# A two-block transformer step on one core: matmul operand tiles and split-weight slots get strides of 2096 and 4112 bytes

## What is computed

```python
h_l = modulate(rms_norm(x, g_mix_norm[l]), sh_a, sc_a)
qa_l, kva_l, kr_l, cb_l, cc_l, ch_l = split_projection(h_l @ w_in[l])
...
x = x + gt_a * merge_heads(att_l, conv_l, g_mix_out[l], w_out[l])
hf_l = modulate(rms_norm(x, g_ffn_norm[l]), sh_f, sc_f)
x = x + gt_f * conv_ffn(hf_l, w_up[l], ffn_conv_w[l], ffn_conv_b[l], w_down[l])
...
z = hn @ w_in
...
x = x + merged @ w_out
hm = rms_norm_2(x, norm_mlp_g)
x = x + jnp.square(jax.nn.relu(hm @ w_up)) @ w_down
```

## Time and profile before

| | |
|---|---|
| median of 2 runs | 2871.82 us (2871.63 to 2872.02) |
| the profiled execution's own time | 2872.42 us |
| its span in the trace | 2870.6 us |
| TensorE, matmuls (PE) | busy 2684.6 us, 94%, 21408 entries |
| TensorE, weight loads (PEld) | busy 2571.9 us, 90% |
| VectorE (DVE) | busy 1794.6 us, 63% |
| ScalarE (ACT) | busy 1224.7 us, 43% |
| DMA | 552.93 MB, mean 193 GB/s |
| mean granted TensorE clock | 0.959 of full speed |

### The profile page before, as it was taken

The page is one execution under the profiler, slowest core; times in us unless marked ns, Lnnn a source line. Parts: engine busy times, 40 slices in busy tenths (PEclk is TensorE's granted clock), DMA queues, the critical chain, the costliest instruction groups (busy, mean ns, idle before and its releaser), DMA issues.

```text
span 2870.6 us, 52211 instructions
## 1 busy us (share of the span) xinstructions
PE 2684.6 (94%) x21408; PEld 2571.9 (90%) x21408; DVE 1794.6 (63%) x2056; ACT 1224.7 (43%) x1407; POOL 20.8 (1%) x24
## 2 busy tenths in 40 slices
PE   4959977768899999999999999999999999999998
PEld 3659975348899999999999999999999999999998
DVE  3988965678766776576556455555555555555554
ACT  2733331223455554354454344444444443434433
POOL 0000000000000000000000000000000000000000
PEclk9989987769999999999999899999999999999999
DMA  4958953427566656656556455566556666666562
GB/s 156 384 195 315 331 171 120 147 88 282 188 191 201 195 182 204 192 163 220 183 171 186 130 173 166 161 188 199 196 178 184 191 197 192 190 196 193 196 206 103
DMA packets 288834, 552.93 MB, mean 193 GB/s; under 512 B 19434, under 2 KB 28632, under 8 KB 288024
## 3 DMA queue, kind: packets, MB, share of 16 engines
q1 hardware_dynamic: 287416, 548.10, 59.2%
q10 hardware_dynamic: 1248, 2.42, 0.3%
HBM read 548.35 MB, written 2.10 MB: 192 GB/s over the span
## 4 chain that ended last, share of the span: by engine, by line
PE 86%; DVE 9%; issue 2%; ACT 2%; DMA 1%; ACTq 1%; DVEq 0%; SPq 0%
PE half L1627 25%; PE half L1629 25%; PE half L1628 25%; DVE wlo L909 2%; PE half L1683 1%; DVE acc L931 1%; PE half L1661 1%; PE half L1663 1%; DVE acc L928 1%; PE half L1662 1%; DVE tmp L1233 1%; DMA raw<-in_w_ada 1%; PE half L1832 1%; PE half L1821 1%; PE half L1822 1%
## 5 line engine op out<-in xcount | busy, mean ns | idle before, releaser
L909 DVE TENSOR_TENSOR wlo<-raw,whi 128x1024 fp32r<-128x1024 f32 (+2 forms) x917 | 1096.7, 1209 | 815.8 <-ACT whi L511 813.6
L511 ACT ACTIVATE whi<-raw 128x1024 fp32r<-128x1024 f32 (+2 forms) x917 | 952.5, 1048 | 1195.0 <-PE half L1629 1033.6
L1627 PE MATMUL half<-hf,whi 128*128 128x256 f32 x2400 | 663.9, 277 | 6.2 <-DVE hf L986 5.1
L1628 PE MATMUL half<-hf,whi 128*128 128x256 f32 x2400 | 663.4, 276 | 0.0
L1629 PE MATMUL half<-hf,wlo 128*128 128x256 f32 x2400 | 663.4, 276 | 0.0
L1627 PE MATMUL half<-hid,whi 128*128 128x256 f32 x1712 | 474.0, 277 | 0.0
L1628 PE MATMUL half<-hid,whi 128*128 128x256 f32 x1712 | 473.4, 276 | 0.0
L1629 PE MATMUL half<-hid,wlo 128*128 128x256 f32 x1712 | 473.4, 276 | 0.0
L1627 PEld LDWEIGHTS half<-hf,whi 128*128 128x128 f32 x2400 | 451.4, 188 | 7.0 <-issue 5.5
L1629 PEld LDWEIGHTS half<-hf,wlo 128*128 128x128 f32 x2400 | 451.3, 188 | 0.0
L1628 PEld LDWEIGHTS half<-hf,whi 128*128 128x128 f32 x2400 | 451.2, 188 | 0.0
(11 more groups left out here) (253 smaller groups left out, 3092.0 us busy)
## 6 DMA issues: line engine op xcount, KB each, us to landing
raw<-in_w_up SPq DMA_DIRECT2D x288, 512.0 KB, 4.4
raw<-in_w_in SPq DMA_DIRECT2D x216, 512.0 KB, 4.1
raw<-in_w_down SPq DMA_DIRECT2D x212, 512.0 KB, 4.1
raw<-in_w_ada SPq DMA_DIRECT2D x192, 512.0 KB, 5.7
raw<-in_w_out SPq DMA_DIRECT2D x64, 512.0 KB, 4.7
raw<-in_w_proj_a SPq DMA_DIRECT2D x16, 512.0 KB, 3.7
raw<-in_w_proj_b SPq DMA_DIRECT2D x16, 512.0 KB, 4.2
raw<-in_w_up SPq DMA_DIRECT2D x16, 384.0 KB, 3.5
```

The lines of the kernel that those rows point to most:

```text
L511: A(whi[:, s, 0:elems], raw[:, c, 0:elems], ACT.Copy).then_inc(s_hi_ready, 1)
L909: V.tensor_tensor(wlo[:, s, 0:elems], raw[:, c, 0:elems], whi[:, s, 0:elems].bitcast(F32), ALU.subtract).then_inc(s_drained, 1)
L1627: mm(o, hi, x[:, 0:T], start=(k == 0 and b % 2 == 0), stop=False, skip_group_check=True)
L1628: mm(o, hi, x[:, T:2 * T], start=False, stop=False, skip_group_check=True)
```

## The change

`SKEW` (12 elements, 48 bytes) is added to the row of each block k of the ten moving-operand tiles, and `SLOT_SKEW` (4 elements, 16 bytes) to each slot of `whi` and `wlo`. The added elements are never written or read. The stride from k to k + 1 becomes 2096 bytes and the one from slot to slot 4112 bytes. Since `whi` and `wlo` grow by 64 bytes each, `wlo` starts 64 bytes later (82112) and all behind it 128 bytes later; tiles that lie behind a skewed one move further (`hf` and `h2` at 124864, `hid0` at 158400, `hid1` and `merged` at 191936). The instructions of every engine, their order, counts, shapes and waits are the same ones; only addresses differ. `raw`, into which the DMAs write, keeps its place and stride, and `qn` and `kvn` keep their strides.

```diff
+SKEW = 12
+SLOT_SKEW = 4
...
-        whi = sb("whi", [P, NSPLIT, CW], F32R)
-        wlo = sb("wlo", [P, NSPLIT, CW], F32R)
+        whi = sb("whi", [P, NSPLIT, CW + SLOT_SKEW], F32R)
+        wlo = sb("wlo", [P, NSPLIT, CW + SLOT_SKEW], F32R)
...
-        h1 = sb("h1", [P, KT, 2 * T], F32R, scope=sc)
+        h1 = sb("h1", [P, KT, 2 * T + SKEW], F32R, scope=sc)
...
-        hctx = sb("hctx", [P, KT, 2 * T], F32R, scope=sc2)
+        hctx = sb("hctx", [P, KT, 2 * T + SKEW], F32R, scope=sc2)
...
-        mix = sb("mix", [P, KT, 2 * T], F32R, scope=sc)
+        mix = sb("mix", [P, KT, 2 * T + SKEW], F32R, scope=sc)
...
-        hf = sb("hf", [P, KT, 2 * T], F32R, scope=sc)
-        hid = [sb(f"hid{i}", [P, HT, 2 * T], F32R, scope=sc) for i in range(2)]
+        hf = sb("hf", [P, KT, 2 * T + SKEW], F32R, scope=sc)
+        hid = [sb(f"hid{i}", [P, HT, 2 * T + SKEW], F32R, scope=sc) for i in range(2)]
...
-        h2 = sb("h2", [P, KT, 2 * T], F32R, scope=sc)
-        heads2 = [sb(f"heads2_{i}", [P, HEADS, 2 * T], F32R, scope=sc) for i in range(2)]
+        h2 = sb("h2", [P, KT, 2 * T + SKEW], F32R, scope=sc)
+        heads2 = [sb(f"heads2_{i}", [P, HEADS, 2 * T + SKEW], F32R, scope=sc) for i in range(2)]
...
-        merged = sb("merged", [P, KT, 2 * T], F32R, scope=sc2)
+        merged = sb("merged", [P, KT, 2 * T + SKEW], F32R, scope=sc2)
```

## The result

The changed kernel takes 2949.35 us (2948.81 to 2949.88) against 2871.82 us: a ratio of 1.027, with a 95% interval of 1.0226 to 1.0314. The forecast was 2835 us, and the range ended at 2910.

A forecast was written before the change was run, and what follows sets the result against it. Behind 758 us the matmul count times their distance was taken as the bound. Fast matmuls gaining 25 us and slow ones 12, with all else zero, gave 2872.4 less 37, 2835 us; range 2786 to 2910.

The forecast's parts named there:

- What bounds the kernel: Behind 758 us, time is the number of matmuls times the distance between two starts; ahead of it TensorE shares the bound.
- The costs put at zero: DMA writes to raw, and ScalarE and VectorE writing and reading skewed slots: zero cost.
- the pair from which the prediction took its -7 to +7 ns: VectorE instructions of one size: 1218 ns on sq, 32 bytes off a multiple of 64, 1225 ns on xt.
- the term of the distances: Products behind 758 us: skewed addresses hinder load and stream less, all go at 111.7 ns, gaining 37 us.
- The two ends of the term: Products behind 758 us: 109.0 ns everywhere gains 82 us; the slow distance everywhere costs 67 us.
- 111.7 ns of the 8-column matmuls: Distance of full-clock matmuls with almost no stream beside the load, taken as the forecast for all products.
- The rival "no change": Loads set the pace and the rest is a handshake that knows no address: 2872 us, chance 0.30.
- The rival "slower": Operands fetched in 64-byte lines, skewed stretches touch one more: 85 us, 2957 us; chance 0.16 for 2939 to 2957.
- the seventeenth line: 1024 bytes starting inside a 64-byte line touch 17 lines instead of 16; the extra one costs 6.7 ns.
- the case beside it: The skew knocks every product into the slow distance: 2939 us, within the 0.16 for 2939 to 2957.
- The floor: Skill's N/2.4 + 2.5 ns, 109.2 ns for 256 columns; trace said to disagree at 113.3; best end 79 us by it.
- The range: From 2786 us, just under the full gain, to 2910, half way to the slow distance everywhere plus a little.

The follow-up runs named there:

- the whole-line skew: Both skews set to 64 bytes, where the changed kernel has 48 and 16; 2946.66 us, ratio 1.0234 to the kernel before.

## Why the prediction was wrong, point by point

**What bounds the kernel** was right. Behind 758 us the time is the number of matmuls times their distance, and 4.4 ns on each is the whole 75 us. The early stages moved by 1.7 us.

**The costs put at zero** were right. The splits on VectorE and ScalarE with skewed slots take 1223 and 1059 ns as before. It is these rows that show it; the pair from which the prediction took its -7 to +7 ns is weaker than it says, since `xt<-tmp,xt` reads `tmp`, which also lies 32 bytes off a multiple of 64.

```profile
L911 DVE TENSOR_TENSOR wlo<-raw,whi 128x1024 fp32r<-128x1024 f32 x880 | 1067.2, 1223 | 874.8 <-ACT whi L513 872.7 <-issue 0.4
...
L513 ACT ACTIVATE whi<-raw 128x1024 fp32r<-128x1024 f32 x880 | 925.5, 1059 | 1230.9 <-PE half L1631 1072.8 <-PE half L1665 55.7 <-DMA raw<-in_w_in 34.4
```

**The step that failed** is the term of the distances: "If loads and streams hinder each other when they are in the same part of a 64-byte line, then they do it now at each matmul and will do it afterwards at some of them." That took the present standing of the operands for the worst one, and from it came the gain of 37 us, where the runs show a loss of 75. They do hinder each other by address, but the kernel before has its moving tiles 64 bytes (modulo 128) from the weights, and none of the eight standings that were tried was better; its opposite, 0, costs 120.0 ns. All skews by 16 to 64 bytes lost. The two ends of the term, -82 us and +67 us, were read from rows rightly, and the 67 us (everything at the slow distance) came close to the loss. The choice between them was the error: 111.7 ns of the 8-column matmuls is what a load costs with hardly a stream beside it, and says nothing of what a stream adds elsewhere. The 8-column matmuls still follow at 111.7 ns in the timeline of the changed kernel, twelve steps in 1.34 us:

```profile
1650.58 0.25 PE L1973 MATMUL half<-whi,h 128*128 128x8 f32 x1
...
1651.92 0.25 PE L1973 MATMUL half<-whi,h 128*128 128x8 f32 x1
```

There were hints. The fast pace held for thousands of matmuls in a row, and 88% of all products had it, so there was much to lose and little to win: 1.7 ns down to the load alone, 4.5 ns up to a pace that the trace already showed.

**The rival "no change"** leaned on `qn`, 256 bytes off modulo 512 and equally fast. Row and conclusion were right for multiples of 256, and the text said that nothing else had been tried. The Trainium skill's "SBUF — State Buffer", section "Who interferes with whom", gives TensorE two independent read ports and says that it never waits on anyone; the kernel with the gap of 64 bytes, at 120.0 ns instead of 113.3 with no instruction changed, disagrees as far as the two operands of TensorE go.

**The rival "slower"** named a price, 85 us, that was near, and a mechanism, the seventeenth line, that the whole-line skew refuted. Its 2957 us lie 8 us over the result; the case beside it, every product in the slow distance at 2939 us, lies 10 us under it. Neither was the mechanism: the changed kernel isn't locked in the even 117.8 ns but wanders around 118.3.

**The floor.** The 109.2 ns from the Trainium skill's "TensorE: Matmul & The Clock Gate", section "Back-to-back issue gap", is what that section gives for a matmul alone; of pairs of load and matmul it says that both set the distance. So the 113.3 ns don't speak against it, as the prediction has it.

**The range** ended at 2910 on the ground that the slow distance everywhere was unlikely. Together these two cases had a chance of 0.16.

## What to carry to other kernels

Before spreading addresses of a matmul's moving and stationary operands, find out from the timeline what the present distance of starts is, and whether it is even; one that is even and near the cost of the load alone has little to win. Try the layout as an experiment of its own: a gap of 64 bytes between two tiles cost 3.8% here, in a kernel in which no instruction changed. And any edit that shifts tiles against the weights by a number of bytes that isn't a multiple of 256 can change the time of a kernel like this one by some per cent, so it must be told apart from the effect of the edit itself.

## What the runs showed of the hardware

All of this is for dense float32r matmuls of 256 moving columns with a weight load each, at full clock.

- The distance of starts depends on how far apart moving and stationary operand begin: 113.3 ns at best, 120.0 ns at 64 bytes from that, 117 to 120 ns in between, but for two products at 80 bytes with 113.35, and moving both together changes nothing. Shifts by 256 bytes gave the same distances; shifts by 128 didn't (64 and 320 bytes at 120.0 ns, 448 at 118.7). What part of the chip does this no row shows.
- At the best standing there are two even paces, 113.3 and 117.8 ns. An interruption by other matmuls, or a step by 128 bytes, chooses between them. Why the step of the weights led to the fast pace and that of the moving tiles to the slow one is open.
- With the same addresses in each group the distances repeat within 1 ns at nearly all places, while VectorE, ScalarE and DMAs work beside them at changing times. But addresses alone don't set them: `h2` at 80 bytes went at 113.35 ns in two products and at 118.7 in most others.
